# Logits from the residual itself, residual in halves, and the last tile normalised on GpSimd, in the output projection of a two-block transformer kernel

## The chip, the cores and the metric

The kernel runs on one core of a Trainium2 chip. Its time is in device microseconds (us): the time of one execution, as the median of a few runs. TensorE (PE) multiplies matrices, VectorE (DVE) and ScalarE (ACT) work on SBUF and on PSUM, GpSimd (POOL) works on SBUF and issues part of the DMAs, SyncE (SP) issues the others. Engines run on their own and wait for each other through semaphores.

## The reference

Two blocks follow each other on 512 tokens of 1024 columns. The first block has two layers with mixers and 16 experts; the second has one layer and is not touched. Layer 0 works on 512 tokens and on 256 context tokens, layer 1 on the 512 tokens alone. What matters here is the end of the mixers and the choice of tokens:

```
x_new = x + g1 * (concatenate([ya, yb, yc, yd]) @ w_out)
h2 = rms_norm(x_new, n2) * (1 + sc2) + sh2
x_new = x_new + g2 * expert_choice_ffn(h2, router, w_gate, w_up, w_down)
# expert_choice_ffn: aff = softmax(h @ router); gates, idx = top_k(aff of each expert, cap); xs = h[idx]
# rms_norm(x, g) = x * rsqrt(mean(x * x) + EPS) * g, row by row
```

`g1`, `sc2` and `sh2` are rows of 1024 numbers computed from the condition, one set for the tokens and one for the context.

## The kernel before

The program is a list of stages, and each engine goes through them in order. Around the change they are, in each layer: `attend`, `conv_out`, `w_out`, `route`, `experts`. Most engines enter a stage when ScalarE, VectorE and GpSimd have all finished the one before; `route` is entered by an engine when that engine itself is done, and TensorE waits there for data alone. An engine says that it has finished a stage by a tiny write to `done_mark` (lines 2354, 3203 and 3445).

`w_out` has tiles of 128 tokens, six in layer 0 and four in layer 1. The weights come in two units of 512 output columns, each one load of SyncE (line 864). In `conv_out` TensorE already computes most of the products of the first two tiles, from the same weights (`project_part`, line 1286, is used by both stages), and ScalarE and VectorE split the weights into a rounded and a small part (lines 2042 and 2710). For each tile the order is:

1. TensorE projects both column halves and signals `projected` once.
2. VectorE multiplies by `g1` (2747), adds to the residual `X` (2750); ScalarE squares the row and takes the root (2073, 2074); VectorE takes the reciprocal (2754), and normalises, scales and shifts the row into `h` (2755, 2756).
3. TensorE transposes `h` (`turn_rows`, 1335), ScalarE and VectorE copy one half each out of PSUM (2068, 2738).
4. TensorE multiplies with the router (`logits`, by the helper of line 962).
5. GpSimd stores `h` to the DRAM tensor `h_rows` (3348), in layer 0 also `X` to `moe_rows` (3350).

TensorE's order is written out by hand: project tile i + 1, transpose tile i, logits of tile i - 1. The last tile is projected, normalised, transposed and multiplied with nothing else to do.

`route` works on all logits at once: VectorE subtracts the maximum (2767, 2768), ScalarE exponentiates, VectorE sums, divides (2771 to 2775), and finds the 64 largest of each expert in eight rounds (2785 to 2788). Then GpSimd gathers the rows of the first experts from `h_rows` (3366), and TensorE transposes them (1383) and runs the experts (1406, 1415, 1427, 1434).

SyncE issues all large loads in one fixed order: the two units of `w_out`; the pieces of expert 0's gate and up weights, 1 MB each, as the slots come free; the down pieces of expert 1 when VectorE has finished `w_out`; the down pieces of expert 0 when logits and stores are done; then the pieces of expert 1, 2 and so on, each when its place has been read. A wait of SyncE holds everything behind it. `out_mods`, the rows of `g1`, `1 + sc2` and `sh2`, are loaded by GpSimd at the start of `conv_out` (3338), three per set.

## Time and profile before

| | us |
|---|---|
| median of 3 runs | 3193.59 |
| runs | 3193.59, 3210.1, 3192.15 |
| profiled execution | 3190.8 |
| its span, first to last instruction | 3189.0 |
| TensorE busy in the span | 2960.4 (93%) |
| VectorE / ScalarE / GpSimd busy | 1102.0 / 737.3 / 381.9 |
| mean granted TensorE clock | 0.961 |

Busy times are sums over the span. A matmul of f32 data takes two instructions. The granted clock is a share of 2.4 GHz, so 0.50 is the level of 1.2 GHz. Times in rows are counted from the start of the span; layer 0's `w_out` lies at about 471 to 558, layer 1's at 1412 to 1468.

### The profile page before, as it was taken

Reading aid. Unit: us, or ns where it says so; the run is one execution under the profiler, and the core shown is the slowest. Engines: PE = TensorE matmul, PEld = TensorE weight load, DVE = VectorE, ACT = ScalarE, POOL = GpSimd, SP = SyncE. Lnnn points to the kernel's source line nnn. Section 1 sums busy time; section 2 is a strip of 40 time slices with the busy share of each in tenths; the row PEclk is TensorE's granted clock in tenths of the full one; section 3 lists DMA queues with packets and bytes.
Section 4 is the critical chain, followed back from the end, with each engine's and each line's share of the span. In section 5 each row is a group of like instructions: output and inputs, shape, how many; then the busy total and the mean of one; then the engine's idle time right before and its main releaser. Section 6 shows DMA issues by size and latency. Waiting matters only on the chain.

```text
span 3189.0 us, 50152 instructions
## 1 busy us (share of the span) xinstructions
PE 2960.4 (93%) x21706; PEld 1867.0 (59%) x21706; DVE 1102.0 (35%) x1930; ACT 737.3 (23%) x1393; POOL 381.9 (12%) x494
## 2 busy tenths in 40 slices
PE   6999989699999998986998888999999999999999
PEld 3645556455454475554433343888865568678887
DVE  4124744211111254643222224222424473232242
ACT  3113651000000132641000002222322362222232
POOL 2022620122222121411000000000000000000000
PEclk9998989799999999997999999999999999999999
DMA  8930033899999810037999996122312112231130
GB/s 343 394 134 1 1 145 124 343 402 409 411 406 413 323 56 0 1 139 282 422 423 423 424 423 276 60 106 80 114 48 75 49 38 80 79 111 66 68 145 28
DMA packets 138400, 626.97 MB, mean 197 GB/s; under 512 B 12592, under 2 KB 19776, under 8 KB 82896
## 3 DMA queue, kind: packets, MB, share of 16 engines
q1 hardware_dynamic: 122064, 577.67, 45.0%
q0 software_dynamic: 16128, 46.18, 4.3%
q8 instruction: 172, 2.82, 0.3%
q14 instruction: 36, 0.29, 0.0%
HBM read 607.36 MB, written 16.45 MB: 196 GB/s over the span
## 4 chain that ended last, share of the span: by engine, by line
PE 42%; DMA 10%; DVE 2%; ACT 1%; issue 1%; SPq 0%; POOL 0%; DVEq 0%; ACTq 0%; POOLq 0%
PE bank L962 19%; PE bank L1529 8%; DMA slots<-in_w_up_dram 7%; PE bank L1717 4%; DMA slots<-in_w_gate_dram 3%; PE bank L1406 3%; PE bank L1633 3%; PE bank L1286 1%; PE bank L1650 1%; PE bank L1427 1%; PE bank L1661 0%; PE bank L1456 0%; PE bank L1651 0%; PE bank L1063 0%; PE bank L1064 0%
## 5 line engine op out<-in xcount | busy, mean ns | idle before, releaser
L1406 PE MATMUL bank<-slots,HT 128*32 128x256 f32 x8192 | 482.3, 387 | 48.1 <-DMA slots<-in_w_gate_dram 24.9
L1406 PEld LDWEIGHTS bank<-slots,HT 128*32 128x32 f32 x8192 | 268.9, 112 | 265.7 <-issue 70.9
L962 PE MATMUL bank<-hT_high,chunk_high 128*128 128x512 f32 (+2 forms) x736 | 285.0, 387 | 5.3 <-DVE hT_low L2504 5.3
L962 PE MATMUL bank<-hT_high,low_slots 128*128 128x512 f32 (+2 forms) x736 | 282.8, 384 | 0.0
L962 PE MATMUL bank<-hT_low,chunk_high 128*128 128x512 f32 (+2 forms) x736 | 280.9, 382 | 0.0
L2097 ACT ACTIVATE arena<-bank 128x512 f32<-128x512 f32 x32 | 19.1, 597 | 756.4 <-PE bank L1406 433.8
L962 PE MATMUL bank<-slots,HT 128*128 128x512 f32 (+4 forms) x544 | 180.8, 492 | 7.2 <-issue 5.8
L2847 DVE TENSOR_TENSOR arena<-bank,arena 128x512 f32<-128x512 f32 x32 | 22.1, 692 | 438.8 <-ACT arena L2097 438.8
L962 PEld LDWEIGHTS bank<-hT_high,chunk_high 128*128 128x128 f32 x736 | 139.0, 189 | 32.0 <-DVE hT_low L2504 5.7
L962 PEld LDWEIGHTS bank<-hT_high,low_slots 128*128 128x128 f32 x736 | 138.3, 188 | 29.5
L962 PEld LDWEIGHTS bank<-hT_low,chunk_high 128*128 128x128 f32 x736 | 138.7, 188 | 27.8 <-issue 0.2
L1427 PE MATMUL bank<-arena,HT 128*32 128x512 f32 x1280 | 147.9, 598 | 3.1 <-DVE HT L2842 3.1
L2983 DVE TENSOR_TENSOR arena<-bank,arena 128x512 f32<-128x512 f32 x44 | 30.4, 692 | 346.0 <-PE bank L962 346.0
L962 PEld LDWEIGHTS bank<-slots,HT 128*128 128x128 f32 x544 | 96.4, 193 | 84.7 <-issue 69.6
L1529 PE MATMUL bank<-down_high,ffnT_low 128*128 128x512 f32 x352 | 137.7, 391 | 0.0
L1529 PE MATMUL bank<-down_high,ffnT_high 128*128 128x512 f32 x320 | 125.8, 393 | 0.0
L1529 PE MATMUL bank<-low_slots,ffnT_high 128*128 128x512 f32 x320 | 124.2, 388 | 0.0
L2888 DVE TENSOR_TENSOR X<-X,bank 128x1024 f32<-128x1024 f32 x60 | 70.0, 1207 | 152.2 <-PE bank L1456 152.2
L1415 PE MATMUL bank<-slots,HT 128*32 128x256 f32 x2048 | 122.4, 379 | 0.0
L3315 POOL TENSOR_TENSOR HT<-HT,arena 128x512 f32<-128x512 f32 (+1 forms) x90 | 107.5, 1194 | 74.8 <-ACT arena L1970 64.8
L1233 PE MATMUL bank<-arena 128*128 128x512 f32 (+2 forms) x224 | 100.8, 572 | 9.8 <-ACT HT L1960 7.3
L2170 ACT ACTIVATE arena<-bank 128x512 f32<-128x512 f32 x44 | 26.3, 598 | 355.0 <-PE bank L962 355.0
(453 smaller groups left out, 4866.4 us busy)
## 6 DMA issues: line engine op xcount, KB each, us to landing
slots<-in_w_gate_dram SPq DMA_DIRECT2D x128, 1024.0 KB, 19.0
slots<-in_w_up_dram SPq DMA_DIRECT2D x128, 1024.0 KB, 21.2
arena<-in_w_down_dram SPq DMA_DIRECT2D x80, 1024.0 KB, 24.1
arena<-in_ada_w_dram SPq DMA_DIRECT2D x48, 1024.0 KB, 8.9
X<-in_w_down_dram SPq DMA_DIRECT2D x32, 1024.0 KB, 17.0
slots<-in_w_in_dram SPq DMA_DIRECT2D x15, 2048.0 KB, 8.3
slots<-in_ffn_w_gate_dram SPq DMA_DIRECT2D x10, 2048.0 KB, 7.6
slots<-in_ffn_w_up_dram SPq DMA_DIRECT2D x10, 2048.0 KB, 8.7
```

Source lines behind the costliest of these rows:

```text
L962: mm = pe.matmul(out_, lhsT, rhs, start=(n == 0), stop=(n == len(pairs) - 1))
L1233: mm = pe.matmul(bank[:, 6 + j, lo:hi], V_ext[:, one.kt, group.kind, at_v:at_v + P], p, start=one.first, stop=ends)
L1286: mm = pe.matmul(bank[:, b + j, :], y, part, start=(k == OUT_WHOLE[0]), stop=(k == OUT_LATE[-1]))
L1406: mm = pe.matmul(bank[32 * j:32 * j + 32, 2 + n, 256 * g:256 * g + 256], xT[:, 64 * k + 32 * g:64 * k + 32 * g + 32], columns(w[:, c, :], ...
L1415: mm = pe.matmul(bank[32 * j:32 * j + 32, 4, 256 * n:256 * n + 256], xT_c[:, 32 * k:32 * k + 32], columns(w[:, c, :], j), start=(k == 0 an ...
L1427: mm = pe.matmul(bank[32 * j:32 * j + 32, 5, :], actT[half][:, 2 * q + c, lo:lo + 32], w[:, c, 512 * h:512 * h + 512], start=(q == 0 and c ...
L1529: mm = pe.matmul(bank[:, b, :], x, w_parts[part][:, 512 * half:512 * half + 512], start=(k == 0 and m == 0), stop=(k == F_CHUNKS - 1 and m ...
L1633: mm = pe.matmul(bank[:, j, :], HT[:, k, tile_cols(i)], w[:, k, :], start=(k == 0), stop=(k == KD - 1))
L1650: pe.matmul(bank[:, b, 0:qt * P + P], qT[rows, h, tile_cols(qt)], kT[rows, h, 0:qt * P + P], start=True, stop=False)
L1717: mm = pe.matmul(bank[:, b + n, :], w, x, start=(k == ks[0] and part == 0), stop=(k == ks[-1] and part == 2))
L2888: dve.tensor_tensor(X[:, t, :], X[:, t, :], flat_bank[:, at_spread:at_spread + D], ALU.add).then_inc(sem["spread_taken"], 1)
L3315: pool.tensor_tensor(dst, other, products[:, n % 4, 0:hi - lo], ALU.add).then_inc(sem["tap_added"], 1)
```

## The change

The logits are computed without the normalised row. Since `h2` is `x_new` times a number of the row, times a gain and plus a shift of the columns, the logits are the number of the row times (`x_new` @ (gain * router)), plus (shift @ router). So:

- SyncE loads gain and shift once more, by columns (`out_cols`), in front of the weights of `w_out`; it waits for GpSimd's `attend` before it. There are four such loads in layer 0 and two in layer 1.
- VectorE makes two small products with the router (`router_of`) at the start of `w_out`, and TensorE sums the shift's product over the partitions (`shifts`), once per set.
- TensorE transposes `X` instead of `h`, and signals, takes and frees the projection by column halves. Its order is: half of tile i + 1, transposes of tile i, logits of tile i - 1, other half of tile i + 1. At the end the halves of transposes and logits alternate.
- VectorE works on the residual by halves.
- The last tile is normalised by GpSimd in three operations (`norm_last`), of which two wait until the ranking has taken the logits. The other tiles stay on VectorE.
- `route` first multiplies the logits by the numbers of the rows and adds the shift's products.
- SyncE waits for all stores to `h_rows` before the first down pieces.

```
@@ stages
-            signals=dict(..., projected=tiles, projected_taken=tiles, residual=tiles, out_root=tiles,
-                         rows_ready=tiles, turned_full=tiles, turned_taken=2 * tiles, logits=1, ...
+            signals=dict(..., sent_by_sp=16 * 2 * (tiles // 2 - 1), projected=2 * tiles, projected_taken=2 * tiles, residual=2 * tiles, ...
+                         rows_ready=tiles - 1, logits=1, ...
...
+        router_of = mod[:, 1, 0:4 * KD * EXPERTS].rearrange("p (r a k e) -> p r a k e", r=2, a=2, k=KD)
+        out_cols = mod[:, 1, 4 * KD * EXPERTS:4 * KD * EXPERTS + 4 * KD].rearrange("p (r a k) -> p r a k", r=2, a=2)
@@ sync
+            def load_out_cols(st):
+                sp.wait_ge(sem["gpsimd_finished"], st.number)
+                for row in range(2 if st.layer == 0 else 1):
+                    for n, comp in enumerate((4, 3)):
+                        sp.dma_start(out_cols[:, row, n, :], mods_rows[st.layer][row, comp * D:comp * D + D].rearrange("(k p) -> p k", p=P), allow_slow_non_contiguous=True)\
+                            .then_inc(sem["sent_by_sp"], 16)
...
+                if stage.name == "conv_out":
+                    load_out_cols(stage)
                 if stage.name == "w_out":
                     sp.wait_ge(sem["mixed"], attended)
...
                 sp.wait_ge(sem["vector_finished"], stage.facts["arena_free"])
+                sp.wait_ge(sem["rows_stored"], projected.at("rows_stored", projected.signals["rows_stored"]))
                 load_down(1, 1)
@@ tensor, w_out
+                def project_half(i, j):
+                    if i >= 2 and j == 0:
+                        pe.wait_ge(sem["projected_taken"], st.at("projected_taken", 2 * (i - 1)))
...
+                def turn_half(i, half):
+                    pe.wait_ge(sem["residual"], st.at("residual", 2 * i + half + 1))
+                    pe_may_fill(pe, st, 4 + half, i)
+                    for c in range(4):
+                        mm = pe.transpose(bank[:, 4 + half, tile_cols(c)], X[:, i, tile_cols(4 * half + c)], ident[:, :])
+                    mm.then_inc(sem[f"full{4 + half}"], 1)
+                def logits(i, half):
+                    pe.wait_ge(sem[f"free{4 + half}"], at_bank(st, 4 + half, i))
+                    for k in range(4 * half, 4 * half + 4):
+                        mm = pe.matmul(bank[:, 6, i * EXPERTS:(i + 1) * EXPERTS], HT[:, k, tile_cols(i)],
+                                       router_of[:, i // ST, 0, k, :], start=k == 0, stop=k == KD - 1)
...
+                def shifts():
+                    for row in range(tiles // 2 - 1):
+                        product(bank[:, 6, P + row * EXPERTS:P + row * EXPERTS + EXPERTS],
+                                [(mean_of[:, :], router_of[:, row, 1, k, :]) for k in range(KD)])
+                for i in range(2):
                     for j in range(2):
+                        project_half(i, j)
+                for i in range(last):
                     if i:
+                        project_half(i + 1, 0)
+                    for half in range(2):
+                        turn_half(i, half)
+                    if i:
+                        for half in range(2):
+                            logits(i - 1, half)
+                        project_half(i + 1, 1)
                     else:
+                        shifts()
+                for half in range(2):
+                    logits(last - 1, half)
+                for half in range(2):
+                    turn_half(last, half)
+                    logits(last, half)
@@ scalar, w_out
                 for i in range(tiles):
+                    if i == tiles - 1:
+                        take_turned(i - 1)
+                        take_turned(i)
+                    act.wait_ge(sem["residual"], st.at("residual", 2 * i + 2))
...
@@ vector, w_out
+                dve.wait_ge(sem["sent_by_sp"], st.at("sent_by_sp", st.signals["sent_by_sp"]))
+                for r in range(tiles // 2 - 1):
+                    gain, shift = [out_cols[:, r, n, :].unsqueeze(2).broadcast_to([P, KD, EXPERTS]) for n in range(2)]
+                    dve.tensor_tensor(router_of[:, r, 0, :, :], router[:, st.layer, :, :], gain, ALU.mult)
+                    dve.scalar_tensor_tensor(router_of[:, r, 1, :, :], router[:, st.layer, :, :], float(D // 4), shift, ALU.mult, ALU.mult)
...
+                    for half in range(2):
+                        cols = slice(512 * half, 512 * half + 512)
+                        dve.wait_ge(sem["projected"], st.at("projected", 2 * i + half + 1))
+                        dve.tensor_tensor(h[:, cols], bank[:, b + half, :], out_mods[:, row, cols], ALU.mult)\
+                           .then_inc(sem["projected_taken"], 1)
+                        dve.wait_ge(sem["projected_taken"], st.at("projected_taken", 2 * i + half + 1))
+                        dve.tensor_tensor(X[:, i, cols], X[:, i, cols], h[:, cols], ALU.add).then_inc(sem["residual"], 1)
                     if i:
                         take_turned(i - 1)
+                    if i == tiles - 1:
+                        take_turned(i)
                     dve.wait_ge(sem["out_root"], st.at("out_root", i + 1))
                     step(dve.reciprocal(small[:, 16 + i:17 + i], small[:, 8 + i:9 + i]))
+                    if i < tiles - 1:
                         ...
@@ vector, route
+                step(dve.tensor_tensor(v, logits, per_row(small[:, 16:16 + tiles], tiles, EXPERTS), ALU.mult))
+                for row in range(spans - 1):
+                    shift = bank[:, 6, P + row * EXPERTS:P + row * EXPERTS + EXPERTS].unsqueeze(1)
+                    of_row = v[:, ST * row:min(tiles, ST * row + ST), :]
+                    step.later(dve.tensor_tensor(of_row, of_row, shift.broadcast_to([P, of_row.shape[1], EXPERTS]), ALU.add))
+                step.wait_for(0)
+                step(dve.tensor_reduce(small[:, 0:tiles], v, AX.X, ALU.max))
...
@@ gpsimd
+            def norm_last(st, i, h, row):
+                pool.wait_ge(sem["residual"], st.at("residual", 2 * i + 2))
+                step(pool.tensor_tensor(h, X[:, i, :], out_mods[:, row + 1, :], ALU.mult))
+                pool.wait_ge(sem["logits_taken"], stage_behind(st).at("logits_taken", 1))
+                step(pool.tensor_tensor(h, h, small[:, 16 + i:17 + i].broadcast_to([P, D]), ALU.mult))
+                step(pool.tensor_tensor(h, h, out_mods[:, row + 2, :], ALU.add))
             def w_out(st):
                 for i in range(tiles):
+                    if i == tiles - 1:
+                        norm_last(st, i, h_ring[:, i % ring, :], 0 if i < ST else 3)
+                    else:
+                        pool.wait_ge(sem["rows_ready"], st.at("rows_ready", i + 1))
```

## Rows read from the trace of the kernel before

**Rows 1.** The chain that ended last, by line, with shares of the span:
```profile
PE bank L962 19%; PE bank L1529 8%; DMA slots<-in_w_up_dram 7%; PE bank L1717 4%; DMA slots<-in_w_gate_dram 3%; PE bank L1406 3%; PE bank L1633 3%; PE bank L1286 1%; PE bank L1650 1%; PE bank L1427 1%; PE bank L1661 0%; PE bank L1456 0%; PE bank L1651 0%; PE bank L1063 0%; PE bank L1064 0%
```

**Rows 2.** Busy times of stretches: PE, PEld, DVE, ACT, POOL, PE clock, DMA share, GB/s:
```profile
700.00:800.00 100.00, 100.00 (x1498) 50.05 (x1494) 14.88 (x36) 5.55 (x12) 20.93 (x30) 1.00 1.02 410
...
1600.00:1700.00 100.00, 88.38 (x1124) 39.04 (x1116) 24.88 (x38) 2.39 (x4) 7.14 (x12) 0.98 1.01 423
```

**Rows 3.** TensorE in order of time, layer 1: start, us, line, operation, [idle before]:
```profile
1423.87 1.97 PE L1335 MATMUL bank<-ident,arena 128*128 128x128 f32 x8 [4.89 <-DVE arena L2756]
...
1451.95 1.88 PE L1286 MATMUL bank<-slots,HT 128*128 128x512 f32 x4
...
1454.54 1.86 PE L962 MATMUL bank<-router,HT 128*128 128x16 f32 x16
1458.40 3.60 PE L962 MATMUL bank<-router,HT 128*128 128x16 f32 x16 [2.00 <-ACT HT L2068]
...
1464.57 3.60 PE L962 MATMUL bank<-router,HT 128*128 128x16 f32 x16 [0.78 <-DVE HT L2738]
```

**Rows 4.** VectorE by line from 1400 to 1500: busy us, mean ns | idle:
```profile
L2738 DVE COPY HT<-bank 128x512 f32<-128x512 f32 x4 | 2.7, 685 | 3.2 <-PE bank L1335 3.2
```

**Rows 5.** VectorE in order of time, in `route` of layer 1:
```profile
1468.53 0.23 DVE L2768 TENSOR_TENSOR arena<-bank,small 128x64 f32<-128x64 f32 x1
...
1469.60 0.29 DVE L2775 TENSOR_TENSOR arena<-arena,small 128x32 f32<-128x32 f32 x2
```

**Rows 6.** In order of time: SyncE's loads, GpSimd's marks and loads, TensorE:
```profile
439.66 1.00 SPq L864 DMA_DIRECT2D slots<-in_w_out_dram  x2
442.44 0.11 POOL L3445 MEMSET done_mark<- 128x1 f32 x1
445.48 3.19 POOL L3338 DMA_DIRECT2D arena<-mods_rows  x6 [2.93 <-DVE done_mark L3203]
450.30 3.71 PE L1286 MATMUL bank<-slots,HT 128*128 128x512 f32 x8
...
1372.57 0.09 POOL L3445 MEMSET done_mark<- 128x1 f32 x1
1382.33 0.99 SPq L864 DMA_DIRECT2D slots<-in_w_out_dram  x2
```

**Rows 7.** The loads of line 864 in layer 0, from issue to landing:
```profile
DMA to landing us min/median/max: 7.8/13.6/19.5
```

**Rows 8.** DMA from 1.0 to 3.2 us, and an issue of the page:
```profile
DMA packets 834, 0.01 MB, mean 3 GB/s; under 512 B 834, under 2 KB 834, under 8 KB 834
...
silu_c<-in_c_pair_dram SPq DMA_DIRECT2D x1, 8.0 KB, 2.7
```

**Rows 9.** GpSimd by line and shape: busy us, mean ns | idle:
```profile
L3315 POOL TENSOR_TENSOR HT<-HT,arena 128x512 f32<-128x512 f32 x60 | 84.7, 1412 | 39.9 <-ACT arena L1970 33.0
...
L3304 POOL TENSOR_TENSOR HT<-HT,arena 128x512 f32<-128x512 f32 x8 | 10.2, 1270 | 0.6
...
L3296 POOL TENSOR_TENSOR arena<-arena,conv_a_w 128x512 f32<-128x512 f32 x8 | 8.1, 1032 | 0.0
```

**Rows 10.** Store to landing; gathers at 560 to 620 and 700 to 1000; a gather:
```profile
h_rows<-arena POOLq DMA_DIRECT2D x10, 512.0 KB, 2.9
...
DMA to landing us min/median/max: 2.7/4.2/6.3
...
DMA to landing us min/median/max: 6.0/6.5/7.3
...
1485.77 1.05 POOL L3366 DMA_INDIRECT arena<-h_rows,arena  x1 [17.54 <-DVE arena L2815]
```

**Rows 11.** SyncE's first down pieces in layer 1, and stretches behind them:
```profile
1464.57 4.43 SPq L913 DMA_DIRECT2D arena<-in_w_down_dram  x6
...
1464.57:1485.00 20.43, 4.82 (x22) 4.14 (x22) 14.15 (x58) 1.91 (x5) 0.20 (x2) 0.50 1.01 422
1485.00:1497.20 12.20, 6.28 (x76) 3.35 (x80) 0.92 (x5) 0.00 (x0) 8.91 (x12) 0.59 0.63 230
```

More of the change, by code:

```diff
@@ L305, in block_one_stages @@
         stages.append(Stage(
-            "w_out", l, tiles=tiles,
-            signals=dict(rows_loaded=16 * 3 * (tiles // 2 - 1), projected=tiles, projected_taken=tiles, residual=tiles, out_root=tiles,
-                         rows_ready=tiles, turned_full=tiles, turned_taken=2 * tiles, logits=1, rows_stored=16 * tiles,
+            "w_out", l, tiles=tiles, bank_uses=[0, 0, 0, 0, tiles, tiles, 0, 0],
+            signals=dict(rows_loaded=16 * 3 * (tiles // 2 - 1), sent_by_sp=16 * 2 * (tiles // 2 - 1), projected=2 * tiles, projected_taken=2 * tiles, residual=2 * tiles, out_root=tiles,
+                         rows_ready=tiles - 1, logits=1, rows_stored=16 * tiles,
                          sums_begun=0 if l else 16 * tiles),
-            units=[(weight_unit(a["w_out"][l], (512 * j, 512 * j + 512)), ("projected", tiles - 1)) for j in range(2)]))
+            units=[(weight_unit(a["w_out"][l], (512 * j, 512 * j + 512)), ("projected", 2 * (tiles - 1) + j)) for j in range(2)]))
         stages.append(Stage("route", l, bank_uses=[0, 1, 0, 1],
@@ L897, in _ @@
                         sp.wait_ge(sem["rows_ready"], stage.at("rows_ready", t + 1))
[L898 to L899 removed]
+                        sp.dma_start(out[t * P:(t + 1) * P, :], tail_rows[:, t, :]).then_inc(sem["sent_by_sp"], 16)
+                    sp.wait_ge(sem["sent_by_sp"], stage.at("sent_by_sp", 16 * ST))
                 if stage.name != "experts":
@@ L1329, in turn_rows @@
-                def turn_rows(i):
-                    pe.wait_ge(sem["rows_ready"], st.at("rows_ready", i + 1))
-                    if i:
-                        pe.wait_ge(sem["turned_taken"], st.at("turned_taken", 2 * i))
-                    for k in range(KD):
-                        mm = pe.transpose(bank[:, 4 + k // 4, tile_cols(k % 4)], h_ring[:, i % ring, tile_cols(k)], ident[:, :])
-                    mm.then_inc(sem["turned_full"], 1)
-                def logits(i):
-                    pe.wait_ge(sem["turned_taken"], st.at("turned_taken", 2 * i + 2))
-                    product(bank[:, 6, i * EXPERTS:(i + 1) * EXPERTS],
-                            [(HT[:, k, tile_cols(i)], router[:, st.layer, k, :]) for k in range(KD)],
-                            sem["logits"] if i == tiles - 1 else None)
@@ L1345, in w_out @@
-                project_tile(0)
-                for i in range(tiles):
-                    if i + 1 < tiles:
-                        project_tile(i + 1)
-                    else:
-                        logits(i - 1)
-                    turn_rows(i)
-                    if i and i + 1 < tiles:
-                        logits(i - 1)
-                logits(tiles - 1)
+                last = tiles - 1
+                def project_half(i, j):
+                    if i >= 2 and j == 0:
+                        pe.wait_ge(sem["projected_taken"], st.at("projected_taken", 2 * (i - 1)))
+                    if i == 2 and j == 0:
+                        pe.wait_ge(sem["w_split"], st.at("w_split", 0))
+                    if i >= 2:
+                        project_part(st, i, j, OUT_WHOLE)
+                        project_part(st, i, j, OUT_SPLIT)
+                    project_part(st, i, j, OUT_LATE).then_inc(sem["projected"], 1)
@@ new lines, in turn_half @@
+                def turn_half(i, half):
[9 more added lines that the diff above has]
+                                       router_of[:, i // ST, 0, k, :], start=k == 0, stop=k == KD - 1)
+                    if i == last and half:
+                        mm.then_inc(sem["logits"], 1)
@@ L2766, in route @@
                 v = aff[:, 0:tiles, :]
-                step(dve.tensor_reduce(small[:, 0:tiles], logits, AX.X, ALU.max))
-                dve.tensor_tensor(v, logits, per_row(small[:, 0:tiles], tiles, EXPERTS), ALU.subtract)\
+                step(dve.tensor_tensor(v, logits, per_row(small[:, 16:16 + tiles], tiles, EXPERTS), ALU.mult))
[5 more added lines that the diff above has]
+                step(dve.tensor_reduce(small[:, 0:tiles], v, AX.X, ALU.max))
+                dve.tensor_tensor(v, v, per_row(small[:, 0:tiles], tiles, EXPERTS), ALU.subtract)\
                    .then_inc(sem["logits_taken"], 1)
```

39 lines of the change are left out of this document (9 added, 30 removed).

## The prediction

> **What bounds the kernel now.** I read the chain of waits first, then busy time by stretches, then the two output projections instruction by instruction. The chain carries matmuls of the second block and, of the first block, loads of expert weights [rows 1]. The stretches tell why: in the experts of layer 0 TensorE is busy 100.00 of 100 us; in those of layer 1 88.38, while the DMA engines stand at 1.01 and 423 GB/s [rows 2]. So a shift passes through layer 0's experts with TensorE's start, and through layer 1's with the moment from which the weight stream runs without a gap. The changed stage stands before both, once per layer, and is serial at its end. In layer 1 TensorE waits 4.89 us for the first normalised tile, transposes it slowly (1.97 us), and ends its last projection at 1451.95 + 1.88 = 1453.8; the last logits end at 1464.57 + 3.60 = 1468.2, so the tail is 14.3 us [rows 3]. Layer 0 has the same order of work, and I take the same times for it.
>
> **The tail.** Logits no longer wait for the normalised rows. After the last projection VectorE multiplies a half (I take 0.69 us, what its copy of 512 columns takes), adds it (0.69) and copies its transposed half of the tile before (0.69) [rows 4]; only then, 2.1 us after the projection, can TensorE take up the second half of that tile's logits. Then follow a half of transposes, a copy (0.7), a half of logits, and these three again. At the slow clock, half a tile's logits are 3.60 / 2 = 1.8 and half its transposes 1.97 / 2 = 1.0 [rows 3]: 2.1 + 1.8 + 2 x (1.0 + 0.7 + 1.8) = 10.9. At the fast one (1.86 / 2 = 0.93 [rows 3], transposes half of the slow 1.0): 2.1 + 0.93 + 2 x (0.5 + 0.7 + 0.93) = 7.3. After an idle time of 2.00 us the trace shows 3.60 where 1.86 stood before [rows 3], and the stretch behind it has a granted clock of 0.50, the 1.2 GHz level [rows 11]. The new pause is about as long, so I take 10.9: **-3.4** in each layer; the other end is 3.6 more.
>
> **The start of the stage.** The first transposes need only the residual, so the 4.89 us go and 1.0 us of slow transposes (-5.9). Added are the products with the shift: 16 instructions like a tile's logits, 1.86, in layer 1 and twice that in layer 0. And one tile's transposes and logits, 1.0 + 1.86 = 2.8, now precede the last half projection instead of following it. Layer 1: -5.9 + 1.9 + 2.8 = **-1.2**; layer 0: -5.9 + 3.7 + 2.8 = **+0.6**. In between, each tile has the same TensorE work. Four residual operations of VectorE instead of two lie under the next half tile's projection; the scaling of the router is two or four small operations before the first projection signals. Both cost nothing while projections bound; without this cover they would be about 1 us per layer.
>
> **Route.** The logits are first scaled and shifted: two small operations more in layer 1, three in layer 0, at some 0.27 each (0.23 [rows 5] and a gap): **+0.5, +0.8**.
>
> **SyncE's queue.** Before w_out's weights SyncE now waits until GpSimd has finished `attend`, and issues the column loads. Behind this wait stand both w_out loads and four expert pieces, and TensorE waits for the first. In layer 1 GpSimd was done at 1372.57, the loads went at 1382.33: free. In layer 0 they went at 439.66, but GpSimd was done only at 442.44 + 0.11 [rows 6]. At 0.5 us for an issue, as w_out's two, four loads take 2.0: w_out goes at 444.55, 4.9 late. Its first load landed after 7.8 us, at 447.5, the second after 19.5, 12.1 us later [rows 7], because GpSimd's six row loads, issued from 445.48 on, ran beside it [rows 6]. TensorE took it up at 450.30 [rows 6], 2.8 after landing. Undisturbed it would land after 7.8 again, at 452.35: 2.1 too late. But now the six loads are beside it from its first byte; with 12.1 us, and 1.3 to start (half of the 2.7 that 8 KB take to land [rows 8]), it lands at 458.0: **+7.7**. I take this end, since the issue times coincide.
>
> **GpSimd's store and what stands behind it.** The last tile is a product at the residual, then, after the ranking has taken the logits, a product with the broadcast scale (2 x 1.03, the tap's row) and an addition (2 x 1.27) [rows 9], 4.7 with 0.1 for gaps. The store lands after 2.9 [rows 10]. Only then may SyncE load the eight down pieces; before, four went when VectorE finished the stage. Layer 1: the subtraction ended at 1468.53 + 0.23 [rows 5], now 4.6 earlier and 0.5 later, at 1464.7. 1464.7 + 4.7 + 2.9 = 1472.3, and 1.3 until an empty queue flows (bounds 0 and 2.7): 1473.6 against 1464.57, 9.0 later. Of this the stream today wastes 12.2 x (1 - 0.63) = 4.5 us between 1485 and 1497.2 [rows 11], which the late pieces fill. Layer 1: 9.0 - 4.5 = **+4.5**; 0.9 at the fast clock.
> In layer 0 the pieces aren't needed for long, but the gathers of expert 0 now meet them: 8 x 1,048,576 bytes at 422 GB/s are 20 us of stream, from 8 to 28 us after the logits were taken; the gathers follow 17 us after that point (1485.77 - 1468.76 in layer 1 [rows 5, 10]). A gather lands after 2.7 us at best there today, after 6.5 in the loaded stretch [rows 10]: **+3.8** (other end 0).
> VectorE works beside GpSimd's operations: such a GpSimd operation takes 1.41 instead of 1.27 [rows 9], so I take **+0.2**, up to one whole operation, 2.5. The Trainium skill, "SBUF — State Buffer", section "SBUF: two separate sides", speaks against this part: a VectorE operation with two SBUF inputs and a GpSimd one that reads SBUF exclude each other for a whole instruction. By that rule the products of line 2775, 0.84 us behind the subtraction [rows 5], would wait 1.3 us, or 3.8 if the addition gets in first, and the sum would be up to 3.6 higher.
>
> **Sum.** Layer 0: 7.7 - 3.4 + 0.6 + 0.8 + 0.2 + 3.8 = +9.7. Layer 1: +4.5. Together +14.2 on the profiled execution's 3190.8: 3205.0. The median of the runs shown stands 2.8 above that execution, the lowest 1.4; I say **3206**.
>
> **Rivals.**
> *The serial tail decides: no slower.* Place: w_out's tail in both layers. At the fast clock the tail gives 3.6 more per layer (14.2 - 7.2 = 7.0); if then the weights are in time, 7.7 go: -0.7, 3190. It decides once the weights are under 0.7 late. For it: the new pauses are short (0.7 to 2.1); against it the 3.60 after 2.00 us, and the 7.8 us of an undisturbed load. Chance 0.20.
> *Layer 1 doesn't follow the down pieces.* They are used long after they land; if the next gate and up pieces set the stream and not the backlog, layer 1 gets -4.6 + 0.5 + 0.2 + 3.8 = -0.1 instead of +4.5: 3200. Against: the share of 1.01. Chance 0.18.
> *The column loads are dear.* If the four follow each other at 2.7 each instead of 0.5, w_out is 8.8 later still: 3214; words 512 bytes apart may take more. For: 834 packets for 8 KB [rows 8]. Chance 0.12. The Trainium skill, "DMA: Bandwidth & Descriptors", section "Rules for kernel authors", says that a non-contiguous last dimension becomes one descriptor per element, which is this mechanism; it gives no price.
> *VectorE is held behind GpSimd in the ranking.* A whole addition in layer 0, 2.5 instead of 0.2: 3207. For: 1.41 against 1.27; against: nothing longer in these rows. Chance 0.08; the rule on the ports is this rival.
> *The forecast*: late weights, late store, loaded gathers. Chance 0.42, own range 3197 to 3212.
>
> **Numbers.** The range of 3188 to 3215 takes in all cases but the outer parts of the first and third. 1% is 32 us, about what a measurement of this kernel can tell from no change; no case reaches it. So 0.97 for within, 0.02 slower, 0.01 faster.
>
> **What would show it.** Right: in layer 0 GpSimd's mark, four column loads, w_out about 5 us later than today, and TensorE idle for some 8 us in front of its first product with these weights; logits ending 11 us after the last projection; down pieces issued behind the last store; the DMA share full from there on, without the gap before 1497; first gathers of 6 us. Wrong: weights in time, logits at the 2.4 GHz level, expert 0 starting over 4 us earlier in both layers.

## The result

**Slower by 0.3%.** The changed kernel takes 3210.9 us (median of 20 runs, 3202.17 to 3224.43), the kernel before 3198.03 (20 runs, 3191.61 to 3212.24); the ratio is 1.003, 95% interval 1.0018 to 1.0042. On another chip it was 1.002 (1.0004 to 1.0036; 3208.05 against 3198.29). Forecast: 3206, 3188 to 3215, "within 1%". The prediction took 1% to be about what a measurement of this kernel can tell; with 20 runs of each it told 0.3%. The profiled execution takes 3202.5 with a span of 3200.6; before 3190.8 and 3189.0. So 11.6 us are to be found; forecast for the span: 14.2.

The chain by line, which answers to [rows 1]:

```profile
PE bank L975 19%; DMA slots<-in_w_up_dram 10%; PE bank L1556 8%; PE bank L1744 4%; PE bank L1433 3%; PE bank L1660 3%; PE bank L1299 1%; PE bank L1677 1%; PE bank L1454 1%; SPq L925 0%; PE bank L1688 0%; PE bank L1483 0%; PE bank L1678 0%; PE bank L1076 0%; PE bank L1077 0%
```

The stretches of [rows 2], and the one behind the first down pieces of layer 1, with the columns as there:

```profile
700.00:800.00 100.00, 100.00 (x1538) 51.11 (x1531) 14.39 (x33) 5.55 (x12) 20.90 (x30) 1.00 1.02 408
...
1480.68:1506.84 26.16, 7.73 (x80) 4.16 (x84) 9.20 (x39) 0.00 (x0) 9.00 (x14) 0.53 0.96 379
...
1600.00:1700.00 100.00, 87.10 (x1113) 37.93 (x1108) 24.88 (x37) 1.79 (x3) 7.13 (x12) 1.00 1.01 423
```

The limits are the same: TensorE in layer 0's experts, the DMA engines in layer 1's. The gap of [rows 11] (share 0.63) is gone.

Now layer 0, SyncE, GpSimd and TensorE in order of time, as in [rows 6]:

```profile
442.64 0.11 POOL L3500 MEMSET done_mark<- 128x1 f32 x1
442.77 2.38 SPq L884 DMA_DIRECT2D arena<-mods_rows  x4
445.25 5.46 PE L975 MATMUL bank<-HT,mean_of 128*128 128x512 f32 x8 [5.42 <-DVE done_mark L3247]
445.27 1.27 SPq L866 DMA_DIRECT2D slots<-in_w_out_dram  x2
445.68 3.19 POOL L3382 DMA_DIRECT2D arena<-mods_rows  x6 [2.93 <-DVE done_mark L3247]
460.50 1.22 PE L1299 MATMUL bank<-slots,HT 128*128 128x512 f32 x1 [9.80 <-DMA slots<-in_w_out_dram]
```

SyncE leaves the wait when GpSimd has set its mark, spends 2.38 us on four column loads, and asks for `w_out` 5.6 us later than before. TensorE then stands idle for 9.80 us and begins at 460.50 instead of 450.30. The weight loads themselves have become slow, from issue to landing (7.8/13.6/19.5 in [rows 7]; TensorE waits for the first of the two, the minimum):

```profile
DMA to landing us min/median/max: 15.2/18.4/21.7
```

The end of layer 0's `w_out`: TensorE, VectorE's products of `route`, GpSimd's last tile, SyncE's down pieces.

```profile
554.61 1.88 PE L1299 MATMUL bank<-slots,HT 128*128 128x512 f32 x4
556.32 0.96 PE L1352 MATMUL bank<-arena,HT 128*128 128x16 f32 x8
558.60 1.07 PE L1352 MATMUL bank<-arena,HT 128*128 128x16 f32 x8 [1.31 <-DVE HT L2767]
560.83 1.89 PE L1352 MATMUL bank<-arena,HT 128*128 128x16 f32 x8 [0.69 <-ACT HT L2095]
564.43 1.89 PE L1352 MATMUL bank<-arena,HT 128*128 128x16 f32 x8 [0.78 <-DVE HT L2767]
567.76 1.89 POOL L3390 TENSOR_TENSOR arena<-arena,small 128x1024 f32<-128x1024 f32 x1 [7.40 <-DVE arena L2812]
568.54 1.30 DVE L2819 TENSOR_TENSOR arena<-arena,small 128x48 f32<-128x48 f32 x2
569.74 2.34 POOL L3391 TENSOR_TENSOR arena<-arena 128x1024 f32<-128x1024 f32 x1
575.84 2.07 SPq L925 DMA_DIRECT2D arena<-in_w_down_dram  x4
...
595.56 1.11 PE L1410 MATMUL bank<-ident,arena 128*128 128x128 f32 x4 [10.21 <-DMA arena<-h_rows,arena]
```

Half a tile's logits go from 1.07 to 1.89 within the tail, which ends 9.8 us after the last projection. The pair of products starts inside a GpSimd operation and ends behind it. Then TensorE waits 10.21 us for the gather. In layer 1 (the same lines; [rows 3, 5, 10, 11]):

```profile
1460.88 1.88 PE L1299 MATMUL bank<-slots,HT 128*128 128x512 f32 x4
1467.10 1.14 PE L1352 MATMUL bank<-arena,HT 128*128 128x16 f32 x8 [0.69 <-ACT HT L2095]
1469.96 1.89 PE L1352 MATMUL bank<-arena,HT 128*128 128x16 f32 x8 [0.78 <-DVE HT L2767]
1473.80 1.34 DVE L2819 TENSOR_TENSOR arena<-arena,small 128x32 f32<-128x32 f32 x2
1480.68 3.10 SPq L925 DMA_DIRECT2D arena<-in_w_down_dram  x6
...
1498.84 1.10 PE L1410 MATMUL bank<-ident,arena 128*128 128x128 f32 x4 [8.96 <-DMA arena<-h_rows,arena]
```

**One ruler for all kernels.** Single executions of one kernel differ in parts that no edit touches, so I compare them by stretches. The first mark is the start of the statistics' eight products on the first tiles (`HT,mean_of`), which stands before any wait for `w_out`'s weights: 445.05 before, 445.25 after. From it I count the request for the weights ("asked"), the first product with them, the transposes of expert 0's gathered rows and the same mark of layer 1 (all of layer 0). Layer 1 runs from its mark to the first product of block two, block two from there to the end of the span. The kernels are those of the next section; *after_again* and *behind_again* repeat the changed kernel and *cols_behind*, unedited.

| kernel | mark | asked | first product | gathered | layer 0 | layer 1 | block two | span |
|---|---|---|---|---|---|---|---|---|
| before | 445.1 | -5.4 | 5.3 | 137.3 | 943.2 | 573.7 | 1227.1 | 3189.0 |
| changed | 445.3 | 0.0 | 15.3 | 150.3 | 953.9 | 571.0 | 1230.5 | 3200.6 |
| after_again | 443.8 | 0.2 | 17.0 | 152.1 | 957.0 | 571.6 | 1230.3 | 3202.7 |
| cols_behind | 444.4 | -5.4 | 5.3 | 137.8 | 943.3 | 572.7 | 1229.3 | 3189.6 |
| behind_again | 452.8 | -5.4 | 5.3 | 137.5 | 943.3 | 573.2 | 1229.1 | 3198.4 |
| wait_kept | 445.5 | -2.5 | 7.6 | 141.8 | 946.7 | 573.2 | 1229.1 | 3194.5 |
| cols_runs | 444.5 | -0.6 | 11.9 | 147.1 | 950.7 | 571.1 | 1230.4 | 3196.6 |
| cols_twice | 451.1 | 5.4 | 19.5 | 154.6 | 960.3 | 572.6 | 1229.4 | 3213.4 |
| cols_alone | 449.6 | 0.1 | 17.0 | 151.4 | 956.9 | 574.4 | 1236.9 | 3217.8 |
| vec_norm | 445.6 | 0.0 | 13.9 | 147.7 | 953.4 | 574.4 | 1237.2 | 3210.6 |
| vec_norm_early | 449.5 | 0.2 | 15.0 | 150.0 | 953.7 | 573.2 | 1227.5 | 3203.8 |
| cb_gather0 | 449.0 | -5.4 | 5.3 | 133.9 | 943.6 | 572.7 | 1229.2 | 3194.5 |
| cb_gather1 | 454.1 | -5.4 | 5.3 | 137.8 | 943.3 | 586.8 | 1229.1 | 3213.3 |
| cb_split0 | 445.7 | -5.4 | 5.3 | 134.1 | 939.7 | 574.4 | 1237.2 | 3197.0 |

The 11.6 us: 0.2 before the mark, +10.8 in layer 0, -2.7 in layer 1, +3.3 in block two, where the code is the same (the last section comes back to it).

### The profile page after: what moved, and what is told of

Read it like the earlier page. It is cut to its first block, busy times and chain, and to the rows that moved or that the text cites. A ratio compares the mean times of both kernels' runs of the same rounds, so it can differ in the third digit from the quotient of the medians.

```text
span 3200.6 us, 50303 instructions
## 1 busy us (share of the span) xinstructions
PE 2959.5 (92%) x21754; PEld 1864.3 (58%) x21754; DVE 1104.1 (34%) x1957; ACT 737.3 (23%) x1393; POOL 394.7 (12%) x500
## 2 busy tenths in 40 slices
DMA packets 144641, 627.00 MB, mean 196 GB/s; under 512 B 18832, under 2 KB 26016, under 8 KB 89136
## 4 chain that ended last, share of the span: by engine, by line
PE 42%; DMA 10%; DVE 2%; ACT 1%; issue 1%; SPq 0%; POOL 0%; DVEq 0%; ACTq 0%; POOLq 0%
PE bank L975 19%; DMA slots<-in_w_up_dram 10%; PE bank L1556 8%; PE bank L1744 4%; PE bank L1433 3%; PE bank L1660 3%; PE bank L1299 1%; PE bank L1677 1%; PE bank L1454 1%; SPq L925 0%; PE bank L1688 0%; PE bank L1483 0%; PE bank L1678 0%; PE bank L1076 0%; PE bank L1077 0%
## 6 DMA issues: line engine op xcount, KB each, us to landing
slots<-in_w_gate_dram SPq DMA_DIRECT2D x128, 1024.0 KB, 19.5
X<-in_w_down_dram SPq DMA_DIRECT2D x32, 1024.0 KB, 15.2
```

## The experiments

All but *cols_alone* edit the changed kernel; a ratio is to the kernel before on the same chip, with its 95% interval.

**The weights of layer 0.** Four kernels take the 10 us apart. *cols_behind* (with its repeat *behind_again*):

```
-                if stage.name == "conv_out":
-                    load_out_cols(stage)
...
+                if stage.name == "w_out":
+                    load_out_cols(stages[stage.number - 1])      # behind the two weight loads
```

> The changed kernel, but SyncE issues w_out's two weight loads first, without a wait, and only behind them waits for GpSimd and loads the columns (same bytes, same bookkeeping). My theory: the whole 10.0 us by which layer 0's first product with these weights came later (460.50 against 450.30) is the wait and the column loads ahead of them. Then that product is back at 450.5 (w_out issued at about 439.8), expert 0 of layer 0 starts at about 588 instead of 597.7, and the span falls from 3200.6 by 10 to about 3191; layer 1 is unchanged. Rival (the bytes compete wherever they stand: the four column loads of 1,024 words each slow the weights' second load, which lands while they run): first product at 450.5, but a wait of some us in front of the second half, and only 5 us back, 3196.

> The changed kernel with its column loads behind w_out's weights, again. Expected as the first time: 0.997 of the kernel before, 11 to 13 us less than the changed kernel; layer 0 943.3 and layer 1 from 570 to 573 between the same marks.

Measured: 3197.96 us, ratio 0.9973 (0.9959 to 0.9987); again 3198.41, 0.9993 (0.9975 to 1.0011), on a chip where the changed kernel itself had 3208.05, 9.6 more. Layer 0 is back at 943.3 twice, as in the kernel before, 10.7 less than in the profiled changed kernel and 13.7 less than in its repeat. My theory holds; the rival's wait for the second half didn't come, though SyncE's four issues now take 19.59 us:

```profile
438.97 1.00 SPq L866 DMA_DIRECT2D slots<-in_w_out_dram  x2
441.88 19.59 SPq L884 DMA_DIRECT2D arena<-mods_rows  x4
```

*wait_kept* is this kernel with the wait left in front:

```
+                if stage.name == "conv_out":
+                    sp.wait_ge(sem["gpsimd_finished"], stage.number)
```

> Like the run before it (column loads behind w_out's weights), but with the wait for GpSimd kept ahead of the weights. It prices the wait alone; what is left to the 10.0 is the column loads' own. My theory as in the prediction, where the six row loads of GpSimd do the harm: w_out issued at 442.8, both loads share the DMA engines with the rows, so landing at 442.8 + 1.3 + 12.1 = 456.2 and 5.7 us later than in the kernel before; span about 3197. Rival (the column loads are the dear part): weights undisturbed for their 7.8 us, first product at about 451 to 452, span about 3192.

Measured: 3201.73 us, 0.9995 (0.9978 to 1.0011). The weights are asked for at 443.0, 2.9 us before GpSimd's first row load (445.91). Before, they were asked for 5.8 us ahead of it, in the changed kernel 0.4 us. They land after

```profile
DMA to landing us min/median/max: 10.0/15.8/21.6
```

so the first product is 2.3 later than with the wait gone, where my expectation had 5.7; the layer loses 3.4 (4.0 up to the gathered rows). The larger part of the delay comes with the column loads in front. But this kernel is no test of the prediction's step, in which the row loads run beside the weights from their first byte: here the weights kept half of their head start. *cols_runs* keeps everything in front and changes only the words, `rearrange("(k p) -> p k")` to `rearrange("(p k) -> p k")`; the columns loaded are then other ones than the formula wants:

> The changed kernel, with the wait and the four column loads in front of w_out's weights, but each load fills the 128 partitions with runs of 8 neighbouring elements instead of single ones 512 bytes apart: the same 4 KB in 128 runs of 32 bytes instead of 1,024 of 4. The columns are then other elements than the reference wants; that is the part left wrong. Theory: with the wait alone the first product came 2.3 us later than in the kernel before and the layer lost 4.0; what is left of 12.9 is the words: each 4-byte run takes an engine's time as a packet. Then this run is near the one with the wait alone, plus 2 us for four more issues in front of the weights: w_out issued at 444.9, first product at 455, span 3197. Rival (a load's fixed price decides, not its words): no change from 3200.6, first product at 460.

Measured: 3205.48 us, 1.0003 (0.9988 to 1.0018); first product 11.9, gathered rows 147.1. The rows come 5.3 later than with the wait alone and 3.2 earlier than in the changed kernel (5.0 earlier than in its repeat). Both theories had half of it. How much the words add is not sharp: with single words in front and the same request time the first product came 13.9, 15.0, 15.3, 17.0 and 17.0 after the mark (*vec_norm*, *vec_norm_early*, the changed kernel, its repeat, *cols_alone*). *cols_twice* loads every column a second time, into `more_cols` beside the first:

```
-                for row in range(2 if st.layer == 0 else 1):
+                for cols, row in [(c, r) for c in (more_cols, out_cols) for r in range(2 if st.layer == 0 else 1)]:
```

> The changed kernel with every column load made twice, into a second place, ahead of w_out's weights. If the loads themselves have a price each (with 32-byte runs four of them cost 5.5 us more than the wait alone, single words 3.4 more), another four cost some 9 in layer 0: w_out issued at 447.6, first product at 468 to 470, span 3208 to 3210. Rival (what costs is that anything stands in front, once: a first load's latency, or the overlap with GpSimd's six row loads): 2 us for the issues alone, first product at 462.5, span 3203.

Measured: 3216.08 us, 1.0047 (1.0029 to 1.0065); first product 19.5, layer 0 960.3. That is 4.8 above the mean of the two changed executions (955.5), between the theories. The later request alone is as large: SyncE takes the eight issues in 7.76 us and asks for the weights 5.3 later:

```profile
448.64 7.76 SPq L885 DMA_DIRECT2D arena<-mods_rows  x8
456.52 7.75 SPq L867 DMA_DIRECT2D slots<-in_w_out_dram  x2
```

From that request to the first product it is 14.1 us, no longer than with four loads in front (15.2). *cols_alone* puts the wait and the loads into the kernel before, with nothing else of the change:

> The kernel before with one part of the change alone: SyncE waits for GpSimd and makes the column loads (two in layer 1, four in layer 0) in front of w_out's weights; nothing uses them. My theory: this carries the whole slowdown. In layer 0 the first product with the weights comes 15 us after the stage's first statistics product instead of 5.25, the layer takes 943.2 + 12.9 = 956, layer 1 is untouched (573.7); span 3201 to 3202, ratio 1.003 to 1.004. The reordered logits, the late store and the loaded gathers would then cancel among themselves in layer 0. Rival (the harm needs the change's other parts, the half-tile order above all): 5 us or less.

Measured: 3219.65 us, 1.0056 (1.0032 to 1.0080). Layer 0 takes 956.9, as expected, and layer 1 574.4. One part of the change thus carries the whole slowdown. The profiled span came out 16 us over the expectation: 4.5 of that lie before the mark and 9.8 in block two, on which more below. The ratio's interval takes in the expected 1.004.

**What the weights meet on the way.** SyncE's loads run on the queue q1, GpSimd's on q0. Between the request for the weights and the landing of their first load the traces of *wait_kept*, of *cols_runs* and of the changed kernel show, in packets, MB and share of the engines' time:

```profile
q0 software_dynamic: 193, 0.73, 17.9%
q0 software_dynamic: 451, 1.68, 36.3%
q0 software_dynamic: 682, 2.53, 44.2%
```

In the kernel before there is no such line: the first load had landed before a byte of GpSimd's rows moved. While both run, the engines move some 400 GB/s together, so GpSimd's bytes can be turned into time (an estimate):

| kernel | first load landed after | GpSimd's MB in that time | at 400 GB/s | rest |
|---|---|---|---|---|
| before | 7.8 | 0 | 0 | 7.8 |
| cols_behind | 8.0 | 0 | 0 | 8.0 |
| wait_kept | 10.0 | 0.73 | 1.8 | 8.2 |
| cols_runs | 12.4 | 1.68 | 4.2 | 8.2 |
| vec_norm | 13.8 | 2.32 | 5.8 | 8.0 |
| cols_twice | 14.1 | 2.40 | 6.0 | 8.1 |
| vec_norm_early | 14.8 | 2.63 | 6.6 | 8.2 |
| changed | 15.2 | 2.53 | 6.3 | 8.9 |
| after_again | 16.8 | 3.15 | 7.9 | 8.9 |
| cols_alone | 16.9 | 3.15 | 7.9 | 9.0 |

Nearly all of the longer landing goes with the six row loads, 3.15 MB in all, that the weights used to be ahead of. What is left for the column loads at the landing is 0.2 to 1.2 us; they do the rest of their harm by making the request late. No run moved GpSimd's row loads by themselves, so this split is read from the traces and not shown by an experiment; and a load that is late for another reason also lets more of the rows by. But the weights did begin in time: their first packet of 2,048 bytes starts 1.4 us after the request in the changed kernel, 1.0 before. Only in *cols_twice*, with twice the words ahead, is it 6.5.

**GpSimd's last tile.** *vec_norm* gives it back to VectorE:

```
-                    if i < tiles - 1:
-                        step(dve.scalar_tensor_tensor(h, X[:, i, :], small[:, 16 + i:17 + i], ...))
-                        dve.tensor_tensor(h, h, out_mods[:, row + 2, :], ALU.add).then_inc(sem["rows_ready"], 1)
+                    step(dve.scalar_tensor_tensor(h, X[:, i, :], small[:, 16 + i:17 + i], ...))
+                    dve.tensor_tensor(h, h, out_mods[:, row + 2, :], ALU.add).then_inc(sem["rows_ready"], 1)
...                                   # GpSimd: norm_last goes, and it waits for rows_ready at every tile
```

> The changed kernel, but the last tile is normalised on VectorE in the place where the kernel before has it; SyncE still waits for the last store ahead of the down pieces. My theory: the pair of products in the ranking is back at 0.3 us (1.3 on the shared port, 1.0 less in each layer), but VectorE's two operations of 1.25 us now lie beside half a tile of logits (1.9) and delay the ranking by up to 1; the stores go about 5 us earlier, and so do the down pieces. In layer 0 they then end about 5 us sooner, yet still meet the gather (20 us from 571 on, gather at 586), so its 3 us come back in part. Layer 1 follows expert 0's start and not the pieces: 0 to -2. Span 3197 to 3200. Rival (the down pieces' place sets layer 1): 5 us less there, 3194 to 3196.

Measured: 3211.12 us, 1.0013 (0.9998 to 1.0028), not told apart from the changed kernel. From the end of layer 1's logits to the gathered rows it takes 26.99 us in both (1471.85 to 1498.84; 1473.45 to 1500.44). The pair is back at 0.29 us, and what it gives is spent by the normalisation in front of the ranking:

```profile
1472.93 1.22 DVE L2794 TENSOR_TENSOR arena<-arena 128x1024 f32<-128x1024 f32 x1
...
1474.54 0.23 DVE L2804 TENSOR_TENSOR arena<-bank,small 128x64 f32<-128x64 f32 x1
```

The down pieces went 3.0 us sooner by layer 1's mark (78.5 instead of 81.5 after it, though the logits ended 1.9 later), and layer 1 didn't get faster (574.4 against 571.0): the rival falls. *vec_norm_early* also drops the wait for the last store ahead of the first four pieces:

```
-                sp.wait_ge(sem["rows_stored"], projected.at("rows_stored", projected.signals["rows_stored"]))
                 load_down(1, 1)
```

> As the run before it, and without the wait for the last store ahead of the first four down pieces, which nothing needs once GpSimd does not read the residual (the kernel before had none there). My theory: in layer 0 all eight pieces have gone over before the first gather of expert 0, so the gather lands after about 2.8 us instead of 6.3 and expert 0 starts 3.3 us earlier; in layer 1 the same 3.5; with what the run before gives, 6 to 8 us below the changed kernel: about 3194. Rival (a gather takes long because it comes behind the router's own loads and not behind the pieces): 0 to -1 against the run before it.

Measured: 3206.66 us, 1.0005 (0.9990 to 1.0020). My expectation failed: the pieces still met the gather, for which TensorE waited 10.00 us in layer 0. Four went at 571.15, behind the normalisation, and the other four only at 584.33, behind the stores that now shared the engines with the first. The eight pieces are some 20 us of stream and the gather is issued 20.3 us after the last logits, so what waits for the last tile is hardly over before it. That led to the opposite order.

**Pieces behind the gather.** *cb_gather0* and *cb_gather1* are *cols_behind* with one more wait in front of all eight down pieces, in layer 0 or in layer 1:

```
+                if l == 0:        # in the other kernel: if l:
+                    sp.wait_ge(sem["gathered0"], stage.at("gathered0", 48 - 16 * l))
                 load_down(1, 1)
```

> Column loads behind w_out's weights (as in the first of these runs), and in layer 0 SyncE also waits for the landing of expert 0's first gather before it loads the eight down pieces. My theory: the gather takes 6 us there because it shares the DMA engines with the pieces. Alone it lands after 2.8, expert 0 of layer 0 starts 3.5 us earlier, and since TensorE is busy for all of layer 0's experts the late pieces cost nothing there: 3.5 us below the run with the column loads behind (span 3189.6), 3186; by the medians some 3194. Rival (the gather waits for its own queue or for the stores, not for the pieces): 0.

Measured: 3197.47 us, 0.9989 (0.9972 to 1.0006). The gathered rows come at 133.9 instead of 137.8, so the pieces are what made the gather slow; but layer 0 takes 943.6 all the same. The 3.9 us went into TensorE's next wait:

```profile
582.90 1.10 PE L1412 MATMUL bank<-ident,arena 128*128 128x128 f32 x4 [6.72 <-DMA arena<-h_rows,arena]
585.04 4.94 PE L1435 MATMUL bank<-slots,HT 128*32 128x256 f32 x64 [0.60 <-DVE HT L2883]
614.46 1.94 PE L1435 MATMUL bank<-slots,HT 128*32 128x256 f32 x16 [6.29 <-DMA slots<-in_w_gate_dram]
```

In *cols_behind* the last of these waits is 2.74 us, on VectorE. Expert 1's first piece stands behind the eight.

> The same, but in layer 1 instead of layer 0. The down pieces then go about 14 us later (near 1485 instead of 1471), and the gather is alone, so expert 0 starts 3.5 us earlier. Theory A: from the down pieces on the DMA stream has no gap left in the changed kernel (shares of 0.96 to 1.02 up to the last piece), so what the stream starts later it ends later: the experts of layer 1 end 10 to 14 us later, span 3200 to 3204. Theory B (the prediction's rival: layer 1 follows the start of expert 0, and the pieces' place doesn't matter): 3.5 us less, 3186.

Measured: 3211.5 us, 1.0034 (1.0019 to 1.0048). Layer 1 takes 586.8 instead of 572.7: theory A. The stretches show the DMA engines idle first and full afterwards, while TensorE now starves:

```profile
1460.00:1486.00 26.00, 9.85 (x45) 7.90 (x43) 14.94 (x49) 3.96 (x9) 7.34 (x6) 0.56 0.28 111
1486.00:1500.00 14.00, 4.30 (x36) 2.45 (x40) 4.42 (x21) 0.00 (x0) 7.73 (x11) 0.50 0.36 117
...
1510.00:1600.00 90.00, 72.17 (x1001) 34.63 (x991) 16.95 (x29) 3.67 (x5) 7.03 (x12) 0.92 1.01 422
```

From its first down piece (1495.38) to the first product of block two (1984.17) it needs 488.8 us; the changed kernel 489.5 (1480.68 to 1970.14), the kernel before 497.3 (1464.57 to 1961.87).

*cb_split0* lets four pieces go in front of the gather and four behind it, in layer 0:

```
                 load_down(1, 1)
...
+                if l == 0:
+                    sp.wait_ge(sem["gathered0"], stage.at("gathered0", 48))
                 load_down(0, 0)
```

> Column loads behind w_out's weights, and in layer 0 only the last four of the eight down pieces wait for expert 0's first gather; the first four go at the last store as before. With all eight behind it the gather was alone, but expert 1's gate and up pieces then stood behind 20 us of stream and TensorE waited 6.29 us for one instead of 2.74 on VectorE: the gain of 3.85 was given back. My theory: four pieces take 10 us and are over when the gather goes, the other four leave expert 1's pieces 10 us earlier than eight did; so the gather's 3.5 us are kept, layer 0 (from its first statistics product after w_out's weights are asked for to the same one of layer 1) takes 939.8 instead of 943.3, and the span is 3186; ratio to the kernel before 0.996. Rival (any piece behind the gather is handed to expert 1's first wait): 943.3 and 3189.6 as with the columns alone.

> The changed kernel as it is, beside the two others on one chip, since single executions of one kernel differ by some 5 us in their first 440 us and by 2 us where the TensorE clock falls. Expected: 12 us above the kernel before, ratio 1.003 to 1.004.

Measured: 3195.7 us, 0.9985 (0.9971 to 0.9999), beside 3208.05 and 1.002 for the changed kernel on this chip. Layer 0 takes 939.7, the expected 939.8, 3.6 less than with the columns behind alone; expert 1's wait is 2.83 again. It has the lowest ratio but that of *cols_behind*'s first measurement (0.9973, on another chip), and the shortest layer 0: by the medians 12 us below the changed kernel, and faster than the kernel before by an amount that its interval just separates from none. Its profiled span of 3197.0 missed 3186 for a reason outside the edit: block two took 1237.2 there.

## Why the prediction was right, and where its steps were not

The sum of 14.2 stands against 11.6, the total of 3206 against 3210.9, and the sign and the place (late weights in layer 0) are those of the forecast. That the sum came so close is in part luck: layer 1 was off by 7.2, and 1.1 more in layer 0 and 3.3 in block two, which the prediction had at nothing, made up for 4.4 of it. In layer 0, up to the gathered rows (+13.0 by the ruler, forecast +9.7):

- **Weights late: 12.9, not 7.7; the mechanism was right, the size was not.** *cols_behind*'s logits end 108.1 after the mark, the changed kernel's 121.1 (122.9 in its repeat). At the first product with the weights 10.0 of this is there. They were asked for 5.4 later (forecast 4.9) and landed after 15.2 (forecast 1.3 + 12.1 = 13.4) instead of 7.8; 2.8 was slack, as forecast. So the step "now the six loads are beside it from its first byte" held, and its price was 1.8 too low: by the table above some 6.3 of the 7.4 us are the row loads'. The other 2.9 the sum did not have at all. Behind its 9.80 us of idle time TensorE worked at the 1.2 GHz level, and the first eight products took 5.64 us instead of 3.71, which leaves it some 11.7 late; a second such stretch from 495.2 to 498.5, where *cols_behind* has none in the same work, adds the rest (the repeat has no second one, and loses more at the first). The granted clock is the third number from the end:

```profile
460.50:464.40 3.90, 3.90 (x5) 1.82 (x6) 2.36 (x2) 3.27 (x3) 0.00 (x0) 0.50 1.04 411
...
495.20:498.50 3.30, 3.30 (x7) 1.90 (x6) 2.28 (x5) 1.93 (x4) 0.20 (x1) 0.50 0.78 318
```

  In the changed kernel nobody waited for the second weight load. By edits, at the ends of the logits (112.2 in *wait_kept*, 117.7 in *cols_runs*), the wait is 4.1 of the 12.9, four loads with runs of 32 bytes 5.5, single words 3.4 more (5.2 by the repeat). The rival *the column loads are dear* saw that the loads in front would cost more than their issues, but its mechanism did not come: the four did not follow each other at 2.7, SyncE issued them in 2.38 and asked for the weights 0.1 later. The Trainium skill, "DMA: Bandwidth & Descriptors", section "Rules for kernel authors", names one descriptor per element for such a last dimension, and the trace agrees: the page of the profile counts 144,641 packets instead of 138,400, and six column loads of 1,024 words are 6,144.
- **Tail and start: -4.9, forecast -2.8** (logits' end by the mark, 108.1 in *cols_behind* against 113.1 before). The tail took 9.8 where the step gave 10.9: the clock fell to the 1.2 GHz level inside the tail and not at its first pause. In layer 1 it took 9.1, and with the start -7.3 instead of -4.6. That place moves: from the mark to the start of layer 1's last half of logits the executions of the changed order show 70.5 to 70.8, or 72.7.
- **VectorE beside GpSimd: 1.0, not 0.2.** The pair went from 0.29 to 1.34 in layer 1 and was 1.30 in layer 0, while a GpSimd operation of 1.89 us ran; in *vec_norm*, without one, 0.29. Here the prediction went by a row of GpSimd's side (1.41 against 1.27), and the rule of the Trainium skill, "SBUF — State Buffer", section "SBUF: two separate sides", was nearer with its 1.3, which the prediction had put beside the sum. With it, the end of the logits to the gather's issue came 1.6 later, forecast 1.0.
- **Gathers under load: +3.3, forecast +3.8**, shown by *cb_gather0*.

12.9 - 4.9 + 1.6 + 3.3 = 12.9. Of it the layer lost 10.8, since later parts were shorter by some 2 us; 1.7 of them lie in one stretch of layer 1's first stages (77.1 us from 1186.68 before, 75.4 from 1199.96 after), where the granted clock was 0.87 before and 1.00 after in the first 13 us.

**Layer 1: -2.7, not +4.5.** Here the step failed that lets the layer follow the down pieces. They did go late, at 81.5 after the mark instead of 76.4, 5.1 us (the forecast of 9.0 counts 1.3 to start, and a tail at the slow clock). But the layer ends with the later of two chains: some 471 to 473 us after the gathered rows, or about 489 after the first down piece (no execution was under 488.8). Before, the first chain ended at 471.8 and 497.3 had gone by since the pieces: 8 us of slack, more than the 4.5 of idle DMA time that the prediction read from one stretch [rows 11]. So the layer followed expert 0's start, and for layer 1 the rival *layer 1 doesn't follow the down pieces* (chance 0.18) was right: -7.3 + 1.6 (route) + 3.5 (gather) = -2.2, and 471.3 instead of 471.8 behind it. Its price of -0.1 was off by the tail. In the changed kernel the two chains nearly meet, and *cb_gather1* crosses over: its later pieces cost 14.

The rival *serial tail decides* had its first half right (a tail shorter than forecast) and was beaten by the weights. VectorE was not held for a whole addition.

## What to carry to other kernels

Ask of a small load not only when it is issued but what stands behind it on its queue, and of that large load what it will meet if it starts later: here a head start of 5.8 us over another engine's 3 MB was lost, and by the traces that cost more than the later request itself. Moved two lines down, behind the large weights, the same small loads cost nothing that could be measured. A wait also costs behind its end, when TensorE starts again at the lower clock. When a transfer is late, find the two chains that meet at the stage's end and their slack before pricing the delay; one stretch of idle DMA time is not that slack. Moving traffic out of the way of one wait hands it to the next one, and splitting the batch (*cb_split0*) kept the gain where moving all of it (*cb_gather0*) did not.

## What was not expected of the hardware

**The same load landed after 7.8 to 16.9 us.** It is 2 MB in every kernel. The landing goes with how much of the other queue's traffic moves beside it (0 to 3.15 MB in the table); with the time of that traffic taken off the ten executions lie between 7.8 and 9.0. Single words are slow by themselves: from 443.7 to 446.5, before the weights' bytes begin, the changed kernel shows

```profile
DMA packets 3704, 0.01 MB, mean 5 GB/s; under 512 B 3704, under 2 KB 3704, under 8 KB 3704
...
q1 hardware_dynamic: 3704, 0.01, 72.4%
```

so 72.4% of the time of 16 engines over 2.8 us for 3,704 packets, 8.8 ns of an engine for each packet of 4 bytes.

**The granted clock falls under a busy TensorE.** Three of these executions (*vec_norm*, *cols_alone*, *cb_split0*) took about 1237 us for block two, the others 1227 to 1231, with the same instructions. In *cb_split0* the loss lies in attention, 273.7 us against 265.2 before. Two stretches of it, first of *cb_split0*, then of the kernel before:

```profile
2560.00:2600.00 40.00, 38.53 (x181) 25.04 (x180) 23.61 (x79) 21.50 (x59) 0.00 (x0) 0.83 0.01 4
```

```profile
2560.00:2600.00 40.00, 38.52 (x224) 26.19 (x222) 27.86 (x89) 24.37 (x69) 0.00 (x0) 1.00 0.00 1
```

Both are busy for 38.5 of 40 us, and the one was granted 0.83 of the clock on average and got through 181 products where the other had 224 (the stretches are the same by time, not quite the same work). What sets it off stays open, but by the table it is not drawn afresh each time: the three with 1237 are the three whose layer 1 took 574.4, and all three with a layer 1 of 571.0 to 571.6 took 1230.3 to 1230.5. So the 3.3 us of block two stand in the changed kernel's repeat as well, and a small shift before a stage may be what picks its clock; no run tests this. It is worth 8 us of a single execution, more than any term here but the weights, and the time before the first mark differs by up to 10 us as well (443.8 to 454.1). That is why single spans could not decide between these kernels, and the stretches could.
